# A fused mixer, expert and four-branch kernel: weights' rest, sums and rounded squares moved in the layers, last scalings all on VectorE

## The reference, cut to what matters

```python
def second_block(x, c, ...):
    for layer in range(2):
        h = rmsnorm_2(x, norm_g[layer]) * (1.0 + scale) + shift
        proj = jnp.einsum('bld,de->ble', h, w_in[layer])
        (aq, af, ai, ag, rq, rk, rv, rg, mz, mxbc, mdt, gq, gk, gv, gg, glr) = split(proj)
        y_a = hgrn2_branch(aq, af, ai, ag, lower_bounds[layer], ...)      # 4 heads
        y_b = retention_branch(rq, rk, rv, rg, ...)                       # 4 heads
        y_c = ssd_branch(mz, mxbc, mdt, ...)                              # 2 groups
        y_d = gla_branch(gq, gk, gv, gg, glr, ...)                        # 4 heads
        x = x + gate * einsum('ble,ed->bld', concat(y_a, y_b, y_c, y_d), w_out[layer])
    return rmsnorm_2(x, final_g)

def hgrn2_branch(q_in, f_in, i_in, g_in, lower_bound, onorm_g):
    log_f = logaddexp(log(lb), log1p(-lb) + log_sigmoid(f_in))
    k = -expm1(log_f)
    o = chunked_vector_decay(silu(q_in), k, i_in, log_f)
    return group_rmsnorm(o, onorm_g, heads) * silu(g_in)
```

## Time and profile before

| | us |
|---|---|
| median of 3 runs | 3407.12 |
| lowest, highest | 3405.99, 3411.69 |
| the profiled execution: time | 3409.59 |
| the profiled execution: span, first to last instruction | 3407.7 |
| busy: TensorE, VectorE, ScalarE, GpSimd | 3335.2, 2140.3, 1585.9, 200.0 |
| mean granted TensorE clock | 0.991 |

### The profile page before, as it was taken

One profiled execution on the slowest core, in us unless ns is written; L12 is line 12 of the kernel. 1 busy time (PEld: TensorE's weight loads), 2 busy tenths in 40 slices (PEclk: granted clock), 3 DMA queues, 4 the chain that ended last, 5 costly groups with the idle time before them and its releaser, 6 DMA issues. The chain is left out here.

```text
span 3407.7 us, 55618 instructions
## 1 busy us (share of the span) xinstructions
PE 3335.2 (98%) x23758; PEld 2765.4 (81%) x23758; DVE 2140.3 (63%) x2641; ACT 1585.9 (47%) x1844; POOL 200.0 (6%) x191
## 2 busy tenths in 40 slices
PE   8999999999999998999999999999999999999998
PEld 6987676878888887888888888888778888788886
DVE  6665553469888987665657663554576668753544
ACT  5432111248778884343356543434443355643432
POOL 0000000001101112000011000000000010000000
PEclk9999999999999999999999999999999999999999
DMA  5211541369999996122111111344122111111433
GB/s 221 83 54 55 172 163 67 138 242 404 414 414 416 413 415 256 57 75 87 39 64 57 39 63 50 133 151 142 57 86 70 45 45 57 38 63 50 156 124 110
DMA packets 97244, 492.94 MB, mean 145 GB/s; under 512 B 10920, under 2 KB 11432, under 8 KB 59104
## 3 DMA queue, kind: packets, MB, share of 16 engines
q1 hardware_dynamic: 77216, 417.31, 32.0%
q0 software_dynamic: 14160, 51.55, 4.3%
q10 hardware_dynamic: 5616, 20.45, 1.5%
HBM read 431.43 MB, written 57.84 MB: 144 GB/s over the span
## 5 line engine op out<-in xcount | busy, mean ns | idle before, releaser
L136 PE MATMUL ps<-HH,WS 128*128 128x512 f32 (+1 forms) x2592 | 1035.3, 399 | 9.2 <-DVE WS L1572 7.1
L138 PE MATMUL ps<-HH,WS 128*128 128x512 f32 (+1 forms) x2592 | 1014.2, 391 | 0.0
L137 PE MATMUL ps<-HL,WS 128*128 128x512 f32 (+1 forms) x1952 | 763.8, 391 | 0.0
L136 PEld LDWEIGHTS ps<-HH,WS 128*128 128x128 f32 (+1 forms) x2592 | 487.7, 188 | 118.1 <-DVE WS L1572 11.9
L138 PEld LDWEIGHTS ps<-HH,WS 128*128 128x128 f32 (+1 forms) x2592 | 487.2, 188 | 106.0
L1637 ACT ACTIVATE WA<-ps 128x512 f32<-128x512 f32 x240 | 142.7, 595 | 840.8 <-PE ps L138 817.4
L137 PEld LDWEIGHTS ps<-HL,WS 128*128 128x128 f32 (+1 forms) x1952 | 368.1, 189 | 74.5 <-issue 1.2
L136 PE MATMUL ps<-WAR 128*128 128x512 f32 x768 | 306.9, 400 | 0.9 <-DVE WAR L1366 0.9
L138 PE MATMUL ps<-WAR 128*128 128x512 f32 x768 | 301.2, 392 | 0.0
L1572 DVE TENSOR_TENSOR WS<-RAW,WS 128x1024 fp32r<-128x1024 f32 (+1 forms) x153 | 201.7, 1318 | 122.7 <-ACT WS L1567 122.7
L136 PE MATMUL ps<-WS,HH 128*128 128x256 f32 x896 | 259.6, 290 | 14.3 <-DVE WAR L2561 12.5
(11 more groups left out here) (409 smaller groups left out, 5218.8 us busy)
## 6 DMA issues: line engine op xcount, KB each, us to landing
WR<-in_weu SPq DMA_DIRECT2D x36, 1024.0 KB, 9.1
WR<-in_wed SPq DMA_DIRECT2D x36, 1024.0 KB, 8.9
WR<-in_weg SPq DMA_DIRECT2D x35, 1024.0 KB, 10.4
RAW<-in_wo SPq DMA_DIRECT2D x32, 1024.0 KB, 4.9
WA<-in_wada SPq DMA_DIRECT2D x48, 512.0 KB, 4.5
H<-in_weg SPq DMA_DIRECT2D x23, 1024.0 KB, 10.4
H<-in_weu SPq DMA_DIRECT2D x23, 1024.0 KB, 8.9
H<-in_wed SPq DMA_DIRECT2D x22, 1024.0 KB, 10.1
```

Source lines behind the costliest of these rows:

```text
L136: t.matmul(o, l[0], r[0], start=st, stop=False)
L137: t.matmul(o, l[0], r[1], start=False, stop=False)
L138: return t.matmul(o, l[1], r[0], start=False, stop=sp)
```

## The change

Five edits, all in the second block. The sums behind an s unit (`between`) are issued behind the preparation steps of the first core step on every engine that takes part, and their banks are taken at that place. `vector_prep_h` takes the next weights' rest directly behind the size and one step earlier; the sigmoid's product stands one step later, ahead of the sum. ScalarE makes the rounded square straight from PSUM, a second activation for each half, and GpSimd only subtracts; so the wait for the rounded square's tile is ScalarE's too. All eight last scalings of each half are on VectorE, and SyncE stores them in order. ScalarE's two scalings and GpSimd's two products at the end are gone.

```diff
@@ plan_between / plan_between_banks
             wa.take("r", tag)
-            banks.take("rms", tag, 0)
-            banks.take("rms", tag, 1)
             for k in range(2):
                 wa.take("sq", tag, k)
...
-            for i in range(2):
-                banks.give(("rms", tag, i), ("rms_ln", tag, i))
+
+        def plan_between_banks(U):
+            if KIND[U % 12] != "s":
+                return
+            for i in range(2):
+                brief("rms", ("s", U), i, end=("rms_ln", ("s", U), i))
@@ scalar_outputs
                     a.activation(half(tl("osq", U, n), i), ps("o", U, n, i), ACT.Square).then_inc(*up("osq", U, n, i))
+                    if U % 12 < 11:
+                        if i == 0:
+                            free(a, wa, "orms", U, n)
+                        a.activation(half(tl_rounded("orms", U, n), i), ps("o", U, n, i), ACT.Square).then_inc(*up("osq_hi", U, n, i))
@@ gpsimd_norm
-            free(g, wa, "orms", U, n)
             for i in range(2):
                 sq, hi = half(tl("osq", U, n), i), half(tl_rounded("orms", U, n), i)
                 g.wait_ge(*at("osq", U, n, i))
-                g.tensor_copy(hi, sq).then_inc(*up("osq_hi", U, n, i))
                 g.wait_ge(*at("osq_hi", U, n, i))
@@ vector_prep_h
             vector_logsig_size(v, (U,), f, tl("lse", U))
+            vector_next(v, U, "q")
+            yield
+            v.wait_ge(*at("ksig", U))
             if U >= 12:
-                v.wait_ge(*at("ksig", U))
                 v.wait_ge(*at("lb_sig"))
                 v.tensor_scalar(k, k, LB[:, 8 + h:9 + h], None, ALU.mult).then_inc(*up("kscaled", U))
-            yield
-            vector_next(v, U, "q")
-            v.wait_ge(*at("ksig", U))
             vector_logsig_sum(v, (U,), f, f, tl("lse", U))
@@ plan_units, behind the preparation steps
+                    if c == 0 and U > U0:
+                        plan_between_banks(U - 1)
@@ units
                     next(core)
-                    if c == 0 and U > U0:
-                        between(e, U - 1)
...
                     for _ in range(steps):
                         next(prep)
+                    if c == 0 and U > U0:
+                        between(e, U - 1)
@@ result_sync
-                for k in (0, 1, 4, 2, 3, 5, 6, 7) if i else range(8):
-                    s.wait_ge(*(at("normed_gpsimd", k) if i and k in ON_GPSIMD else at("normed", "fin", k, i)))
+                for k in range(8):
+                    s.wait_ge(*at("normed", "fin", k, i))
@@ result_vector
                 for k in range(8):
-                    if not (i and k in ON_GPSIMD):
-                        vector_normed(v, X, "fin", k, i, p2(0, "fin", k))
+                    vector_normed(v, X, "fin", k, i, p2(0, "fin", k))
@@ result_gpsimd removed, scalar_program
                 scalar_square(a, "fin", k, 1)
-                if k - 1 in ON_GPSIMD:
-                    xs = X[:, k - 1, token_half(1)]
-                    a.wait_ge(*at("squared", "fin", k - 1, 1))
-                    a.activation(xs, xs, ACT.Identity, scale=p2(0, "fin", k - 1)).then_inc(*up("fin_gained", k - 1))
```

More of the change, by code:

```diff
@@ L4585, in output_vector @@
             new_x(1, adding=layer == 1)
-        ON_GPSIMD = (4, 5)
         def result_vector(v, layer, i):
@@ L4727, in gpsimd_program @@
                                 gpsimd_norm(g, U, n)
-            result_gpsimd(g)
         def tensor_program(t):
```

## The result

The changed kernel takes 3385.61 us (median of 4 runs, 3383.08 to 3388.15) against 3407.36 us; ratio 0.9935, 95% interval 0.9924 to 0.9947. A second set gave 3385.85 (5 runs) against 3407.07, ratio 0.9937 (0.9923 to 0.9951). So it is 21 to 22 us faster.

The account below looks back on a forecast made before the run. TensorE, busy 98% of the span, bounds the kernel; gains come from its idle time, half clock and tail. Terms 8.4 + 4.7 + 1.8 + 0.8 = 15.7 us off 3409.6, less 2.5 to the median: 3391.5 us, range 3386 to 3400.5.

Parts of the forecast that it names:

- VectorE's chain gives most of the h units' gain back: Layer 1's h units: TensorE 6.1 us ahead, net only 2.1 each; with layer 0's 0.5 the term is 4.7 us.
- The new waits of 1.2 us at L2019 and 1.76 at L1762: H units: 1.2 us before L2015 in layer 0; 1 to 2 us before L1760 for L1744 in layer 1.
- The sums' order: S units: sums L321 moved behind the next projection step save 0.70 and 3.50 us per layer, 8.4 us in all.
- the root's cover of 1.5 us: After the first s unit: the root would end at 1562.6, 1.5 us before VectorE's scaling L1880 needs it.
- Nothing is given back: Rival: the h units keep 10.2 us instead of 4.7; sum 21.2, time 3385.9 us; chance 0.08.
- The clock takes it back: Rival: new idle time in layer 1's h units or the sums brings half clock, 3 to 7 us; about 3397; chance 0.22.
- the four L321 take 3.62 us at half clock where the first unit's take 1.96: Second s unit's sums: the 1.84 us wait and 1.66 us of half clock both go, 3.50 us per layer.
- 5.1 to 8.4: Ends of the sums' term: 5.1 us if only idle time goes and half clock comes elsewhere, 8.4 us otherwise.
- four stretches of half clock: Range's slow end: the clock rival with four stretches, each worth 1.7 us, put at 3400.5 us.
- 0.9 us at the last L1837: Norm, once a layer: without GpSimd's casts its subtractions end 0.9 us sooner; term 2 x 0.9 = 1.8 us.
- the kept end of 4.4: Upper end of the rounded squares' term: 4.4 us with both of TensorE's norm waits gone (2.6 + 1.8).
- SyncE's stores come in the order of the tiles and follow one by one: Tail: eight undisturbed VectorE scalings end at 3403.0 instead of 3403.8; term 0.8 us.

Follow-up runs that it names:

- i2: The changed kernel with eight instead of six idle-time products ahead of the gathered rows alone; 3386.75 us, ratio 0.9938.
- t1: The kernel before with the last half's stores in tile order, GpSimd's two scalings kept; 3414.07 us in one run, 11.52 us from TensorE's end to span end.
- t2: The changed kernel with the last half's stores in the order of before; 3387.18 us in one run, 10.71 us from TensorE's end to span end.
- i1: The changed kernel with eight instead of six idle-time products ahead of the gathered rows and twelve instead of four ahead of L470; 3388.51 us, ratio 0.9944.

## Why the prediction came out as it did

**Right.** The reading that VectorE's chain gives most of the h units' gain back was the longest argument and holds to 0.1 us a unit: net 2.2, 2.2 and 0.5 for 2.1, 2.1 and 0.5. In layer 0 the 0.5 is partly luck: in three of eight traces with the old code half clock stood behind the 1.6 us wait and the new code saved 2.1. The prediction had taken the full clock there as an argument. The new waits of 1.2 us at L2019 and 1.76 at L1762 stand where they were named. The sums' order removed 0.40, 0.3 and 1.84 us as told, with the root's cover of 1.5 us. "Nothing is given back" (3385.9) named nearly the measured time, but for the wrong reason: these units kept 4.9 us, not 10.2. "The clock takes it back" did not come true at its price of 3 to 7 us. Behind the new waits, up to 1.8 us, half clock stood in two of five traces (3.4 us each, at 2832.3 and at 2953.3 in i2), and the place took no longer, 52.81 and 34.27 us, since TensorE would have waited there anyway. At the moved sums it did take something back: half clock in 3 of 10 places of the five traces, 1.5 us each.

**Wrong: the size of the clock's share at the second sums.** The step "the four L321 take 3.62 us at half clock where the first unit's take 1.96 ... so all of 1.84 + 1.66 = 3.50 us goes", and with it the end "5.1 to 8.4". The rows were one execution's. In two of four traces the half clock lasts 10.2 us and the place takes 3.1 us more. The term, 8.4 for both layers' sums, measures 11.7. Upwards it had no room at all: the half clock's own length was not taken as an unknown. The mechanism, a wait and the clock behind it, was right; its size was not. (The range's other end has a slip too: four stretches of half clock from 15.7 leave 8.9 us, so 3398.2 and not 3400.5.)

**Wrong: the norms.** The step "0.9 us at the last L1837" priced idle time alone. In the changed kernel the idle time goes from 1.4 + 0.9 to 0.28 + 0.72, 1.3 us less, and a half-clock stretch behind the wait, 3.4 us long from 1975.4, goes too. It was in the trace of before (window above), and the prediction spoke of two other stretches only. ScalarE, POOL and TensorE at that norm after the change:

```profile
1961.24 0.59 ACT L1819 ACTIVATE WAR<-ps 128x512 fp32r<-128x512 f32 x1
1961.72 0.61 ACT L1815 ACTIVATE WA<-ps 128x512 f32<-128x512 f32 x1
1962.20 0.62 ACT L1819 ACTIVATE WAR<-ps 128x512 fp32r<-128x512 f32 x1
...
1961.98 2.50 POOL L1852 TENSOR_TENSOR WAR<-WA,WAR 128x512 fp32r<-128x512 f32 x2 [48.31 <-ACT WAR L1819]
...
1962.96 0.47 PE L1840 MATMUL ps<-WAR,OR 128*128 128x512 f32 x1 [0.28 <-ACT WAR L1819]
...
1964.53 0.50 PE L1843 MATMUL ps<-WAR,OR 128*128 128x512 f32 x1 [0.72 <-POOL WAR L1852]
```

GpSimd's two subtractions take 2.50 us together, 1.27 each from start to end, where the second took 1.59: 0.3 of the 0.4 us by which the idle time fell more than forecast. 1.8 us were forecast and 4.2 measured; that this is near the kept end of 4.4 is luck, since that end stood for both waits gone, and 1.0 us of them is still there. The stretch is shown to belong to the part: at layer 0's norm all eight traces with GpSimd's casts have it, none of the eight with the new squares, and doubling the squares (e6) brings it back. At layer 1's norm it is left to chance: half clock in five of eight traces with the casts.

**Wrong: the tail's second half.** The step "SyncE's stores come in the order of the tiles and follow one by one", with the end at the last scaling. The scalings gave the 0.8, and the order another 1.28 (t1, t2): the end is set by the transfers, which run at some 380 GB/s from the first store on, and not by the last scaling. The price of a hole in the queue of stores was never worked out; the high end of 1.3 left it out. With GpSimd's two gone, no scaling is above 0.75 us, and t2's 0.80 is what that saves. By the Trainium skill (SBUF — State Buffer, "SBUF: two separate sides") the port pair that VectorE and GpSimd share goes to the one that starts first. The prediction was right to go by the row: VectorE started first and was stretched all the same, to 1.85 us from 0.74.

**Left open.** Why the same 40 products of 8 columns, without idle time among them, stood ahead of half clock at 2443 in the first trace of before and in all 14 traces of other runs, but in neither of the change itself; t2, i1 and i2, with the same code there, have it, 6.8 us long. It lies in no term; 3.4 us of it cost 1.6 (16.99 against 15.37 us from one product to another), 6.8 us 3.2. So 1.6 us of the first two traces' gap is this draw. Nor were the last 0.2 us at the first s units found (0.98 for 0.70, of which the faster sums are 0.08). What makes one fall of the clock 3.4 us and the next 10.2, and what makes it fall without a wait, was not found either.

## What to carry to other kernels

A wait of TensorE can cost its idle time and a stretch of half clock behind it: at 1.8 us it did in 13 of 14 places, at 1.6 us, in layer 0's h units, in 3 of 8. List every stretch below full clock with the wait ahead of it, and give its length a range upwards, from none to 10 us, since one profile shows one draw. Compare kernels by the time between the same two instructions in several traces: places without half clock came out to 0.1 us, while whole runs of the kernel before scatter over 20. But count every trace that has the code in question, not only those that have it everywhere. At a tail of stores, price the order of the queue and the first store's start, not only the last producer's end: here transfers at some 380 GB/s set the end.

## What was not expected of the hardware

The clock's part of a stall can, it seems, be bought back without removing the stall: with useless products of 1.98 us in a wait of 1.84 us both places ran at full clock, 1.7 to 4.8 us faster, though half clock at another wait took 1.6 us back. The clock also falls without a wait, behind 128 products of 32 columns and four of the GK tile, in 5 of 18 places. And in 71 runs of one program the time ranges over 20 us (3397.46 to 3417.40), with the mean granted clock from 0.995 to 0.988 along with it.
